# Expert weights of a fused two-block kernel: 19 lasting buffer places and two used once, in place of 17

## What is computed

```
def second_block(x, c, ctx, ...):
    ...
    out_c, out_l = mixer(h_c, h_l, angles, last, w_in[l], ..., w_out[l])
    x = x + g1[:, None, :] * out_l
    h_l = modulate(rmsnorm(x, norm2[l]), sh2, sc2)
    x = x + g2[:, None, :] * ec_moe(h_l, w_router[l], w_e_gate[l], w_e_up[l], w_e_down[l])
    return rmsnorm(x, final_norm)

def ec_moe(x, w_router, w_e_gate, w_e_up, w_e_down):
    cap = CAP_FACTOR * T // N_EXPERTS                     # 32 tokens for each of 16 experts
    aff = softmax(x @ w_router)
    g, idx = lax.top_k(aff.transpose(0, 2, 1), cap)
    xs = x[idx]
    a = einsum('becd,edf->becf', xs, w_e_gate)
    u = einsum('becd,edf->becf', xs, w_e_up)
    y = einsum('becf,efd->becd', silu(a) * u, w_e_down) * g
    return zeros.at[idx].add(y)
```

## Time and profile before

| | us |
|---|---|
| median of 3 runs | 1671.54 |
| lowest and highest | 1669.98, 1672.26 |
| span of the profiled execution, first to last instruction | 1670.7 |
| TensorE busy in it | 1512.0 |
| DMA engines' mean rate over the span | 237 GB/s |

### The profile page before, as it was taken

One profiled execution on the slowest core, in us unless ns is written; L12 is line 12 of the kernel. 1 busy time (PEld: TensorE's weight loads), 2 busy tenths in 40 slices (PEclk: granted clock), 3 DMA queues, 4 the chain that ended last, 5 costly groups with the idle time before them and its releaser, 6 DMA issues.

```text
span 1670.7 us, 17753 instructions
## 1 busy us (share of the span) xinstructions
PE 1512.0 (91%) x7552; PEld 1009.6 (60%) x7552; DVE 482.1 (29%) x805; ACT 529.6 (32%) x689; POOL 601.4 (36%) x167
## 2 busy tenths in 40 slices
PE   7999999999999999999999999999987676665765
PEld 6777678877877758887788887678731121121111
DVE  2222333331122233332243445768510000010001
ACT  5246343433424634344344333364310000000000
POOL 5646287734654628774437673010000000000000
PEclk9999999999999999999999999999998898999888
DMA  7534355598453435559725443002889999999996
GB/s 255 177 125 131 125 185 182 181 332 304 152 176 126 140 121 190 178 183 370 284 79 177 151 144 121 1 14 76 353 363 421 422 421 422 421 422 421 422 421 282
DMA packets 125497, 395.39 MB, mean 237 GB/s; under 512 B 6743, under 2 KB 10644, under 8 KB 101228
## 3 DMA queue, kind: packets, MB, share of 16 engines
q1 hardware_dynamic: 123536, 388.66, 62.9%
q0 software_dynamic: 1456, 4.52, 0.8%
q10 hardware_dynamic: 428, 1.10, 0.2%
HBM read 393.19 MB, written 1.05 MB: 236 GB/s over the span
## 4 chain that ended last, share of the span: by engine, by line
PE 72%; DMA 21%; SPq 3%; DVE 2%; ACT 1%; issue 0%; DVEq 0%; ACTq 0%
PE psum L2033 17%; PE psum L2035 17%; PE psum L2034 16%; DMA ring<-in_w_e_up 4%; DMA arena<-in_w_e_down 4%; PE psum L2025 4%; PE psum L1093 3%; DMA arena<-in_w_e_up 3%; DMA arena<-in_w_e_gate 3%; DMA ring<-in_w_e_down 3%; SPq L676 3%; DMA ring<-in_w_e_gate 2%; PE psum L1014 1%; PE psum L2271 1%; PE psum L2161 1%; PE psum L954 1%
## 5 line engine op out<-in xcount | busy, mean ns | idle before, releaser
L599 POOL TENSOR_TENSOR ring_lo<-ring,ring_hi 128x2048 fp32r<-128x2048 f32 x101 | 468.0, 4638 | 351.7 <-ACT ring_hi L580 351.7
L2033 PE MATMUL psum<-ring_hi,hT_lo 128*128 128x512 f32 (+2 forms) x896 | 358.2, 400 | 1.5 <-DVE hT_lo L2289 1.2
L2035 PE MATMUL psum<-ring_hi,hT_hi 128*128 128x512 f32 (+2 forms) x912 | 355.5, 390 | 0.0
L2034 PE MATMUL psum<-ring_lo,hT_hi 128*128 128x512 f32 (+2 forms) x912 | 353.1, 387 | 0.0
L580 ACT ACTIVATE ring_hi<-ring 128x2048 fp32r<-128x2048 f32 x116 | 222.0, 1914 | 357.5 <-DMA ring<-in_w_down 116.8
L1093 PE MATMUL psum<-ring,arena 128*32 128x512 f32 x712 | 204.6, 709 | 62.0 <-DMA ring<-in_w_e_down 22.7
L1093 PE MATMUL psum<-arena 128*32 128x512 f32 x736 | 193.9, 701 | 54.1 <-DMA arena<-in_w_e_gate 17.9
L2035 PEld LDWEIGHTS psum<-ring_hi,hT_hi 128*128 128x128 f32 x912 | 171.3, 188 | 37.4
L2033 PEld LDWEIGHTS psum<-ring_hi,hT_lo 128*128 128x128 f32 x896 | 168.4, 188 | 41.7 <-issue 6.0
L2034 PEld LDWEIGHTS psum<-ring_lo,hT_hi 128*128 128x128 f32 x912 | 172.1, 189 | 33.5 <-issue 0.5
L1093 PEld LDWEIGHTS psum<-ring,arena 128*32 128x32 f32 x712 | 42.4, 125 | 160.5 <-issue 52.9
(11 more groups left out here) (399 smaller groups left out, 1648.1 us busy)
## 6 DMA issues: line engine op xcount, KB each, us to landing
ring<-in_w_in SPq DMA_DIRECT2D x60, 1024.0 KB, 5.1
ring<-in_w_up SPq DMA_DIRECT2D x32, 1024.0 KB, 5.5
ring<-in_w_down SPq DMA_DIRECT2D x32, 1024.0 KB, 5.9
arena<-in_w_e_gate SPq DMA_DIRECT2D x31, 1024.0 KB, 26.7
arena<-in_w_e_up SPq DMA_DIRECT2D x31, 1024.0 KB, 27.0
ring<-in_w_e_gate SPq DMA_DIRECT2D x30, 1024.0 KB, 26.7
ring<-in_w_e_up SPq DMA_DIRECT2D x29, 1024.0 KB, 27.0
ring<-in_w_e_down SPq DMA_DIRECT2D x29, 1024.0 KB, 27.3
```

Source lines behind the costliest of these rows:

```text
L599: eng.tensor_tensor(slot_lo(u), slot(u), slot_hi(u).bitcast(F32), ALU.subtract).then_inc(done, 1)
L2033: pe.matmul(dst, lo(k0 + k), w_hi, start=start and k == 0, stop=False)
L2034: pe.matmul(dst, hi(k0 + k), w_lo, start=False, stop=False)
L2035: last = pe.matmul(dst, hi(k0 + k), w_hi, start=False, stop=stop and k == nk - 1)
```

## The change

- The list of places becomes two: EX_FIRST with 21 places for units 0 to 20, and EX_AGAIN, the same without two of them (ONCE), with 19 places for all units from 21 on. `held_before` gives the unit whose release a later load waits for. `more_slots` has 13 places in place of 9, at MORE_AT.
- The waits before the first loads follow the new places (`first_free`). Unit 0's place is new space at the end of `arena` and has no wait.
- `arena` grows from 27600 to 29696 columns, 8384 bytes of each partition, and the scratch for descriptors goes from 16384 to 8192 bytes.
- The second half of `gatedT_lo` gets a place of its own (25600) where `hT_lo`'s upper half served; `stages`, `pick`, `pickT`, `hid`, `hidT`, `y_ex`, `weighed`, `g_row`, `last_row`, `x_tmp` and the selection's rows lie elsewhere in `arena`. The two places used once (23552 and 21504) lie under `hid` and `hidT`, and under `stages[1]` and `pickT`.
- For the four more semaphores that the places need, others are merged: `lat_n` into `lat_sq`, `lt_full` into `xt_full`, `kpe_sb` and `qpe_sb` into `pe_sb`, `y_half` into `o2_half`, `ht_sb` into `hid_a`, with the counts of the waits raised to match.

```
-EX_SLOTS = [R + 1, R + 2, R + 3, R, R + 4, 0, 4, R + 5, R + 6, R + 7, 1, 5, 2, 6, 3, 7, R + 8]
-RE = len(EX_SLOTS)
+MORE_AT = (27648, 11264, 13312, 15360, 17408, 23552, 3072, 21504, 5120, 7168, 9216, 1024)
+ONCE = (R + 5, R + 7)
+EX_FIRST = [R, R + 1, R + 2, R + 3, R + 4, R + 5, R + 6, 0, 4, R + 7, R + 8, R + 9, 1, 5, R + 10, 2, 6, 3, 7, R + 12, R + 11]
+EX_AGAIN = [s for s in EX_FIRST if s not in ONCE]
+NF, RE = len(EX_FIRST), len(EX_AGAIN)
...
-    return EX_SLOTS[(u - U_EX) % RE]
+    i = u - U_EX
+    return EX_FIRST[i] if i < NF else EX_AGAIN[(i - NF) % RE]
...
+def held_before(i):
+
+    return EX_FIRST.index(EX_AGAIN[i - NF]) if i < NF + RE else i - RE
...
-        arena = sb("arena", [P, 27600])
+        arena = sb("arena", [P, 29696])
...
-        gatedT_lo = in_place("gatedT_lo", "arena", 9792, [4, T])
+        gatedT_lo = [in_place(f"gatedT_lo{i}", "arena", first, [4, T]) for i, first in enumerate((9792, 25600))]
...
-        more_slots = [carve(first, UC, UN) for first in (3584, 11776, 14912, 16960, 1536, 5632, 7680, 9728)]
+        more_slots = [carve(first, UC, UN) for first in MORE_AT]
         more_slots.append(hT[:, :, :].rearrange("p k t -> p (k t)").rearrange("p (c n) -> p c n", n=UN))
...
-            def slot_free_for(i):
-
-                if i >= RE:
-                    return U_EX + i - RE
-                s = EX_SLOTS[i]
-                return U_OUT + (s % R1 if s < R else 1)
+            def first_free(s):
+
+                if s in (R + 1, R + 2, R + 3):
+                    sp.wait_ge(raw_full, 2 * MH)
+                elif s == R + 4:
+                    sp.wait_ge(num_full, MH - 1)
+                elif s in (R + 5, R + 6):
+                    sp.wait_ge(num_full, MH)
+                elif s in (R + 7, R + 8, R + 9):
+                    sp.wait_ge(turn_full, FULL + 6)
+                elif s == R + 10:
+                    sp.wait_ge(slots_free, unit_done(U_OUT + 1))
+                elif s == R + 11:
+                    sp.wait_ge(gb_full, 2)
+                elif s == R + 12:
+                    sp.wait_ge(lg_full, 2)
+                elif s < R:
+                    sp.wait_ge(slots_free, unit_done(U_OUT + s % R1))
 
             for i in range(EX_UNITS):
                 u, src = U_EX + i, expert_unit(i)
-                if i < 2:
-                    sp.wait_ge(raw_full, 2 * MH)
-                elif i < 4:
-                    sp.wait_ge(num_full, MH - 3 + i)
-                elif i == 4:
-                    sp.wait_ge(hn_a, 9)
-                elif i in (7, 8):
-                    sp.wait_ge(turn_full, FULL + 6)
+                if i < NF:
+                    first_free(EX_FIRST[i])
                 else:
-                    sp.wait_ge(slots_free, unit_done(slot_free_for(i)))
-                if i == RE - 1:
-                    sp.wait_ge(lg_full, 2)
+                    sp.wait_ge(slots_free, unit_done(U_EX + held_before(i)))
...
-                last = split_product(DB[1 + n][:, t, :], tokens(hT_hi, t), tokens(hT_lo, t), UC, u, start=False, stop=True)
+                last = split_product(DB[1 + n][:, t, :], tokens(hT_hi, t), gated_low, UC, u, start=False, stop=True)
...
-    nc = bacc.Bacc("TRN2", target_bir_lowering=False, num_devices=1)
+    nc = bacc.Bacc("TRN2", target_bir_lowering=False, num_devices=1, dynamic_dma_scratch_size=8192)
```

More of the change, by code:

```diff
@@ L192, in ring_slot, with ring_round @@
         return u % R1
-    return EX_SLOTS[(u - U_EX) % RE]
+    i = u - U_EX
+    return EX_FIRST[i] if i < NF else EX_AGAIN[(i - NF) % RE]
+def ring_round(u):
+    i = u - U_EX
+    return 1 if i < NF else 2 + (i - NF) // RE
+def held_before(i):
+    return EX_FIRST.index(EX_AGAIN[i - NF]) if i < NF + RE else i - RE
 def build(nc, w, out):
@@ L389, in build @@
         af, ab, Gf, Gb = [hT_flat[0:8, UN * i:UN * (i + 1)] for i in range(4)]
-        more_slots = [carve(first, UC, UN) for first in (3584, 11776, 14912, 16960, 1536, 5632, 7680, 9728)]
+        more_slots = [carve(first, UC, UN) for first in MORE_AT]
         more_slots.append(hT[:, :, :].rearrange("p k t -> p (k t)").rearrange("p (c n) -> p c n", n=UN))
-        stages = [carve(13888, KC, P), carve(19008, KC, P)]
-        pick = carve(20032, TT, NE * CAP)
-        pickT = carve(21056, EG, T)
-        hid = carve(22080, 2, UN)
-        hidT = carve(23104, KC, P)
-        y_ex = carve(24128, D)
-        weighed = carve(26176, TT, NE * CAP)
-        chosen, count, place = [carve(23104 + T * i, T)[0:NE, :] for i in range(3)]
-        g_row = carve(25152, D)
-        last_row = carve(26176, D)
-        x_tmp = carve(13888, TT, UN)
+        stages = [carve(19456, KC, P), carve(21504, KC, P)]
+        pick = carve(20480, TT, NE * CAP)
+        pickT = carve(22528, EG, T)
+        hid = carve(23552, 2, UN)
+        hidT = carve(24576, KC, P)
+        y_ex = carve(25600, D)
+        weighed = carve(25600, TT, NE * CAP)
+        chosen, count, place = [carve(25600 + T * i, T)[0:NE, :] for i in range(3)]
+        g_row = carve(0, D)
+        last_row = carve(26624, D)
+        x_tmp = carve(20032, TT, UN)
         small = consts[:, at["dilated"][0]:at["dilated"][0] + 1152]
@@ L435, in build @@
         row_in = sem("row_in")
-        more_in = [sem(f"more_in{i}") for i in range(RE - R)]
+        more_in = [sem(f"more_in{i}") for i in range(NF - R)]
         h2_high = sem("h2_high")
@@ L745, in tensor_block2 @@
             pe.wait_ge(sig_sb, 2)
-            pe.wait_ge(lat_n, 6)
+            pe.wait_ge(lat_sq, 13)
             for k in range(3):
@@ L749, in tensor_block2 @@
                     last = pe.transpose(flat[2][:, k * T + t * P:k * T + (t + 1) * P], q_lat[:, t, k * P:(k + 1) * P], ident)
-            last.then_inc(lt_full, 1)
+            last.then_inc(xt_full, 1)
             pe.wait_ge(xt_sb, 6)
@@ L786, in tensor_block2 @@
                 last.then_inc(qt_full, 1)
-            pe.wait_ge(qpe_sb, 6)
+            pe.wait_ge(pe_sb, 13)
             pe.wait_ge(kv_a, 8)
@@ L792, in tensor_block2 @@
             last.then_inc(qt_full, 1)
-            pe.wait_ge(kpe_sb, 7)
+            pe.wait_ge(pe_sb, 7)
             pe.wait_ge(kv_v, 8)
@@ L1023, in out_unit @@
                         between()
-                    last = split_product(DB[1 + n][:, t, :], tokens(hT_hi, t), tokens((gatedT_lo, hT_lo)[kh], t), UC * kh, u, start=kh == 0, stop=kh == 1)
+                    last = split_product(DB[1 + n][:, t, :], tokens(hT_hi, t), tokens(gatedT_lo[kh], t), UC * kh, u, start=kh == 0, stop=kh == 1)
                     if n == 1 and kh == 1 and t == 0:
@@ L1051, in tensor_block2 @@
                 u = U_OUT + 2 + n
+                gated_low = lambda k, t=t: gatedT_lo[1][:, k - UC, t * P:(t + 1) * P]
                 if t == 0:
@@ L1236, in vector_block2 @@
             tb = xn_flat[:, 128:256].rearrange("p (t d) -> p t d", t=TT)
-            rotate(key, cos2, sin2, ta, tb, halves, kpe_sb, 0)
+            rotate(key, cos2, sin2, ta, tb, halves, pe_sb, 0)
             xm_half(1, (6, 7, 0, 1))
-            dve.wait_ge(lt_full, 2)
+            dve.wait_ge(xt_full, 10)
             for k in range(2):
@@ L1287, in vector_block2 @@
                         if half == 1 and k == 1:
-                            ins.then_inc(qpe_sb, 1)
-                dve.wait_ge(qpe_sb, 3 * t + 2)
-                dve.tensor_tensor(dst, qa, qb, ALU.add).then_inc(qpe_sb, 1)
-                dve.wait_ge(qpe_sb, 3 * t + 3)
+                            ins.then_inc(pe_sb, 1)
+                dve.wait_ge(pe_sb, 3 * t + 9)
+                dve.tensor_tensor(dst, qa, qb, ALU.add).then_inc(pe_sb, 1)
+                dve.wait_ge(pe_sb, 3 * t + 10)
             for n in range(1, 4):
@@ L1456, in low_gated @@
                 k = slice(4 * half, 4 * half + 4)
-                to = (gatedT_lo[:, :, :], hT_lo[:, 4:8, :])[half]
-                dve.tensor_tensor(to, src.rearrange("p (k t) -> p k t", k=4), hT_hi[:, k, :].bitcast(F32), ALU.subtract).then_inc(turn_lo, 1)
+                dve.tensor_tensor(gatedT_lo[half][:, :, :], src.rearrange("p (k t) -> p k t", k=4), hT_hi[:, k, :].bitcast(F32), ALU.subtract).then_inc(turn_lo, 1)
             mask_rows(0)
```

33 lines of the change are left out of this document (14 added, 19 removed).

## The result

| | median, us | runs | ratio to before, 95% interval |
|---|---|---|---|
| before, in the same session | 1670.76 | 4 | |
| after | 1652.20 | 4 (1650.21 to 1654.78) | 0.9893 [0.9881, 0.9905] |

The change makes the kernel 18.6 us faster. The direction was right; the 8.6 us that came on top need a second mechanism, which the prediction does not have.

What follows compares the result with a forecast made beforehand. TensorE was taken to bound the early part, the DMA stream of expert weights the end. Span 1670.7 - 10.0 = 1660.7 us, all other terms 0, plus 0.84 us to the median: 1661.5 us, range 1659.5 to 1666.0.

Steps and rivals of the forecast that it cites:

- The stream account: Expert weight loads: each unit in before TensorE gives the first place back saves 2.50 us at the end.
- the term of -10.0 us: Expert weight loads: four extra units hidden in holes, 171 to come at 1216.6 us, -4 x 2.50 us.
- Semaphores that now share a count, and small buffers that moved ... 0 us: All engines: rows the same but for names, merged counts rise in program order, so 0 us.
- a TensorE that is later before 1153: Sign that the prediction is wrong: TensorE before 1153 us later than it was.
- Holes: DMA gaps before the closed stream, about 6 and 8 us: the first smaller, the one before 1216.6 about 4 us.
- Depth: Expert stream after its start: ring of 19 in place of 17 lets SP issue earlier; 0 us, up to 1 kept.
- tail: Last loads, L1093, L1128 and norm: order and sizes the same, 0 us; 2.4 us kept for a low clock.
- w_gate: Unit 0's load beside it may land it up to 2.5 us later; first reader at 1049.4, 0 us.
- Rival (c): Small scratch makes GpSimd wait at 747.48 us (L1912 to L1920): time up to 1732 us; chance 0.05 with other slowdowns.
- Rival (b): End of the kernel: places, not bytes, set the pace, so the end stays, 1668 to 1672 us; chance 0.05.
- Rival (a): Part of the gain lost in gaps or a low clock on the tail: 1663.5 to 1665.9 us; chance 0.10.
- The unit's price: Expert stream: 1.0486 MB at 419 GB/s is 2.50 us; 358 GB/s would give 2.93 us and -11.7 us.

Runs made afterwards that it cites:

- late unit 0: The changed kernel, 21 places, with the first expert unit held back until the raw scores like the three after it: 1652.29 us, 0.9884 [0.9869, 0.9899].

## Why the prediction was wrong

- **The stream account held.** With 21, 19 and 17 places the stream measured 431.7, 436.7 and 441.7 us, 2.50 us for each unit. In the profiled executions the term of -10.0 us was right to a tenth. In the medians four places brought 8.2 us (1660.46 with 17 places to 1652.29 with 21 and a late unit 0, in one session), 0.53% or 9 us by the ratios.
- **The failed step is "Semaphores that now share a count, and small buffers that moved ... 0 us".** The text looks at each engine's rows of instructions, finds them the same, and sets the price of everything else at 0. The same instructions on operands that lie elsewhere were not the same: `arena`'s new size moved all of `ring`, `x`, `xn`, `hT` and the constants from 64 bytes past a multiple of 256 to a multiple. The sum has no term for that; it measures -8.4 us when done alone and +10.5 when undone alone. 10.0 from the places + 8.5 from the pitch = 18.5, and 18.6 was measured; with medians that scatter by a microsecond or two, the last tenth is luck. The diff showed it in the line of `arena`'s size.
- **The range failed for the same reason.** It was made from the bounds of the terms that were listed. Among its signs of being wrong stands a TensorE that is later before 1153, but none that it is earlier. "Slower" had a rival about the scratch, "faster than forecast" had none, though half of the chain that ended last is in L2033 to L2035, and nobody asked what in the change could touch those.
- **Holes.** The first expert load was forecast near 1025 and came at 1016.66, for the missing term. The 22nd was forecast at about 1215.5 and came at 1203.0: 7.9 us for the missing term, and 4.6 in the stretch behind w_out, where before's profiled execution, from which the forecast was read, had a lower granted clock than after's. The hole ahead of the stream was to shrink to about 4 us and shrank to about 2.5. It decides nothing, as the version with a late unit 0 shows.
- **Depth, tail, w_gate: 0 us each**, right. The stream moves 420 GB/s against 419, and 16.60 + 1.90 + 2.79 us at the end against 16.61 + 1.91 + 2.79; the loads in the stream take 27 us to land, as before.
- **Rival (c), the scratch**: refuted, 1.0001 [0.9991, 1.0010]. The Trainium skill, "DMA: Bandwidth & Descriptors", section "SWDGE vs HWDGE vs iDMA", says that loads issued from SP never touch that scratch. This run agrees as far as its time shows. **Rival (b)**, an end that is not the stream's, is refuted by the 2.5 us per unit. **Rival (a)**, gaps that cost 2 to 4 us, did not come: the release-to-landing time shrank by the full 10.0.
- **The unit's price.** The row's 2.50 us held. The estimate of 2.93 us goes by the 358 GB/s that the Trainium skill names for HBM in "DMA: Bandwidth & Descriptors", section "Where 436 GB/s comes from". The trace does not agree: the streams here moved 419 to 428 GB/s, and the measurement decides.

## What to carry to other kernels

When a change alters the size of one buffer, write down where every buffer behind it begins, modulo 256 bytes, before and after, and treat the whole work of the engines on those buffers as touched. Place the stationary and the moving operands of a matmul-bound stage at like offsets modulo 256; here 192 unused bytes in each partition did as much as three more buffer places of 1 MB. In a stretch that the DMA engines bound, count the units in before it closes: each was worth its transfer time here, 2.50 us, whether its place lasts or is used once. And compare two profiled executions part by part, with the granted clock of each part beside it, before a difference of their spans is put down to a change.

## What the hardware showed that was not expected

- The pitch of 128x512 split products is 227.6 ns when `arena`, `ring` and `hT` begin at like offsets modulo 256 bytes (0, 64 and 128 were tried), and 229.2 to 232.7 ns when they don't. The timeline's lengths don't show it, the mean durations by 3 or 4 ns of 390 to 400, and the busy time of the whole span mixes it with the granted clock (1499.2 and 1509.5 us in two aligned versions).
- A closed stream of 1 MB loads moves 421 or 422 GB/s with `ring` 0 or 64 bytes past a multiple of 256, and 426 to 428 with `ring` 128 past: 5 us in 430. The packets of such a load take 309 ns in place of 314, and those of the next one to three loads as well, wherever they go.
- Half the descriptor scratch costs nothing with 1456 packets on GpSimd's queue.
